# Latent attention: the reciprocals of the softmax sums spread over rows by two fp32r products of ones with diagonal blocks, in place of plain fp32 products

## The chip, the cores and the metric

One core of a Trainium2 chip runs the whole program. The metric is the device time of that core in microseconds (us), lower is better. Before the change three runs gave 3945.37, 3948.91 and 3950.83 us, median 3948.91.

## What is computed

A two-layer backbone over 1024 latent and 256 context tokens. Each layer runs three head groups side by side (a long convolution, retention, latent attention), an output projection and an MLP. The change touches only the attention with its 8 heads:

```python
s = jnp.einsum('bqhd,bkhd->bhqk', qi, k, preferred_element_type=jnp.float32)
p = jax.nn.softmax(s, axis=-1).astype(v.dtype)
return jnp.einsum('bhqk,bkhd->bqhd', p, v)
```

Keys and queries have 96 rows, values 64, keys are 1024 latent and 256 context tokens. In layer 0 context tokens are queries too (they see only the 256 context keys); in layer 1 they are not.

## The kernel before, in words

All products are made in "fp32r": an operand is split into a high part and a low part, each of which the TensorE takes at one pass, and three products (high by high, high by low, low by high) are summed in PSUM. They appear as L152, L153 and L154, the lines of the helper `three_pass`. A product of plain fp32 operands is taken by the TensorE as two instructions for one in the code.

`phase_latent` works on units (p, s, t): pair of heads p (0 to 3), head s in the pair, tile t of 128 queries. Layer 0 has 80 units (10 tiles, the last two of context), layer 1 has 64. Two units in a row are a couple, 72 couples in all. Each engine runs a loop over steps j and handles several units at different stages in it, in an order written out by hand:

- TensorE in step j: scores of unit j in two parts (512 and 768 keys); transposes of the probabilities of units j-2 and j-1 (L2031), which need a free PSUM bank of a ring of four; half of the products with the values of a couple (`weigh`, L2051); and, if the deck has one at this step, a product that makes keys, values or queries of the next pair (`make`). In odd steps `weigh` ends with the products of L2059.
- VectorE in step j: maximum of scores, part 0 (L1923); low parts of probabilities of unit j-2 (L1943); maximum, part 1 and the scaled maximum (L1927); the rest of the low parts; in odd steps `invert` (L1936 adds the two partial sums, L1937 takes the reciprocal).
- ScalarE: high parts of probabilities (L1767), copies of made products out of PSUM (L1748), the couple's output (L1775 to L1777), the exponentials (L1757).
- GpSimd (POOL in the profile): splits what was made into high and low parts (`split`, L1823 to L1847), converts the next pair's weights (`weights`, L1806 to L1809), and multiplies each couple's output by the reciprocals (`norm`, L1856 and L1859).

The softmax is divided by its sums at the very end. The sums of a couple lie as two columns of 128 partitions; the output lies with queries along its columns. So L2059 turns the reciprocals: the column, broadcast to 64 columns, is the stationary operand, the identity matrix the moving one, in plain fp32, once for each unit of the couple. The result, 64 rows of equal values, is copied out at L1775 as `att_rec`.

The semaphore `inverted` tells TensorE that a couple's reciprocals are there, `weighed` tells the others that its last product is done. `invert` of a couple is in VectorE's step 2m+3, the products that use it in TensorE's step 2m+5. `made_in` is the deck: in which step each of the next pair's keys, queries and values is made. It starts with step 5 of each pair's period of 20 (layer 0) or 16 (layer 1) steps and takes one item a step. The raw weights of the next pair are loaded by SyncE and converted by GpSimd in step 3 of a period.

Of the kernel before, what the change touches and what calls it, by code (L numbers as in the profile page):

```python
# [19 lines left out]
F32 = mybir.dt.float32  # L20
F32R = mybir.dt.float32r
ALU = mybir.AluOpType
# [3 lines left out]
P = 128  # L26
# [20 lines left out]
MLA_V = 64  # L47
# [35 lines left out]
class Chain:  # L83
# [6 lines left out]
    def link(self, eng, ins):  # L90
        self.count += 1
        ins.then_inc(self.sem, 1)
        eng.wait_ge(self.sem, self.count)
# [1441 lines left out]
LAT_QW, LAT_KVW = PAIR * HEAD_W, PAIR * (MLA_NOPE + MLA_V)  # L1535


def latent_weights(kit, l, q, p):


    first = p == 0
    uq_raw, ukv_raw = kit.at("uq_raw", [P, 2, LAT_QW], 187 if first else 130), kit.at("ukv_raw", [P, LAT_KVW], 191 if first else 132)
    w_raw = kit.sig("lat_w_raw", 16)
    q.dma_start(uq_raw[:], kit.io["mla_w_uq"][l, p].rearrange("(t p) n -> p t n", p=P)).then_inc(w_raw.sem, 16)
    q.dma_start(ukv_raw[:], kit.io["mla_w_ukv"][l, p]).then_inc(w_raw.sem, 16)
# [11 lines left out]
def phase_latent(kit, l):  # L1557
# [14 lines left out]
    SUM_RING, Q_SLOTS, RAWS = 8, 3, 2  # L1572
    uq_raw = [kit.at("uq_raw", [P, 2, LAT_QW], kb) for kb in (187, 130)]
    ukv_raw = [kit.at("ukv_raw", [P, LAT_KVW], kb) for kb in (191, 132)]
    rot, rope_part = kit.at("rope_rows", [P, SEQ], 70), kit.at("rope_part", [P, 2, 512], 193)
# [14 lines left out]
    kr = kr_wide[:, KR_AHEAD:, :]  # L1590
# [3 lines left out]

    mx = kit.at("att_max", [P, 2, 8], 202.5)
    sums, rinv = kit.at("att_sums", [P, 2, SUM_RING], 202.75), kit.at("att_rinv", [P, SUM_RING], 203)
    psf = ps[:].rearrange("p a b -> p (a b)")
    SCALE = MLA_QK ** -0.5
    T_BANK, T_RING, O0 = 3, 4, 7 * 512
# [6 lines left out]
    per_pair = PAIR * per_head  # L1606
# [20 lines left out]
    for p in range(1, PAIRS):  # L1627
        deck = [("k", p, 0, c) for c in range(3)] + queries(p, 0) + [("v", p, 0, c) for c in range(3)] + queries(p, 1)
        made_in.update({(p - 1) * per_pair + 5 + i: m for i, m in enumerate(deck)})
    later_makes = [made_in[j] for j in sorted(made_in)]  # L1630
# [38 lines left out]
    kr_ready = kit.sig("lat_kr_ready")  # L1669
# [29 lines left out]
    with nc.Block() as block:  # L1699
        @block.sync  # L1700
        def _(sp):
            sp.dma_start(rot[MLA_NOPE:P, :], io["rope_rows"]).then_inc(rot_in.sem, 16)
            sp.wait_ge(kr_ready.sem, kr_ready["kr"])
            latent_weights(kit, l, sp, 1)
            n_tok = len(q_tiles) * P
            for p in range(PAIRS):
                if p + 2 < PAIRS:
                    sp.wait_ge(w_lo.sem, w_lo[p + 1])
                    latent_weights(kit, l, sp, p + 2)
                sp.wait_ge(normed.sem, normed[num[(p, PAIR - 1, q_tiles[-1])] // 2])  # L1710
                row = 2 * HY_W + p * P
                sp.dma_start(kit.cat_dram[row:row + P, 0:n_tok], att[:, p % 2, 0:n_tok]).then_inc(stored[p % 2].sem, 16)
            for s in range(2):
                sp.wait_ge(stored[s].sem, stored[s].total)
# [161 lines left out]
        def _(dve):  # L1876
            link = kit.dve_chain.link
            dve.wait_ge(w_hi.sem, w_hi["first"])
            dve.tensor_tensor(ukvl[:], ukv_raw[0][:], ukvh[:].bitcast(F32), ALU.subtract)
# [50 lines left out]
            def invert(m):  # L1930

                n_parts, at = len(keys(units[2 * m])), 2 * m % SUM_RING
                dve.wait_ge(exped.sem, exped[(2 * m + 1, n_parts - 1)])
                total = sums[:, 0, at:at + 2]
                if n_parts == 2:
                    link(dve, dve.tensor_tensor(total, total, sums[:, 1, at:at + 2], ALU.add))  # L1936
                dve.reciprocal(rinv[:, at:at + 2], total).then_inc(inverted.sem, 1)  # L1937

# [30 lines left out]
        def _(pe):  # L1969
# [65 lines left out]
            def weigh(m, half):  # L2035
# [17 lines left out]
                if half == 1:  # L2053

                    pe.wait_ge(inverted.sem, inverted[m])
                    r = s * MLA_V
                    for i in range(2):
                        at = (2 * m + i) % SUM_RING
                        last = pe.matmul(psf[r:r + MLA_V, O0 + (2 + i) * P:O0 + (3 + i) * P],  # L2059
                                         rinv[:, at:at + 1].broadcast_to([P, MLA_V]), kit.ident[:], start=True, stop=True)  # L2060
                    last.then_inc(weighed.sem, 1)
# [1011 lines left out]
def build(nc, io, phases=None):  # L3073
    with ExitStack() as ctx:
# [5 lines left out]
        kit.stat = kit.small("stat", [P, 4, 20])  # L3080
        kit.ones = kit.small("ones", [P, P])
        kit.mla_gain = kit.small("mla_gain", [P, 3])
# [4 lines left out]
        kit.ret_gcol = kit.small("ret_gcol", [P, DEPTH, RET_H])  # L3087
        kit.ret_pos, kit.ret_lg = kit.small("ret_pos", [P, 4]), kit.small("ret_lg", [P, 8, DEPTH * 2 * RET_H])
        kit.ret_dm_dram = nc.dram_tensor("ret_dm_scratch", (DEPTH, P, RET_H, P), F32).ap()
        kit.spec_dram = [nc.dram_tensor("spec_scratch", (DEPTH, P, SEQ // 2 // P, 2, 4 * HY_W), F32).ap(),  # L3090
# [130 lines left out]
```

## Time and profile before

| | before |
|---|---|
| median of three runs | 3948.91 us |
| the profiled execution | 3948.27 us, of which the span is 3946.4 us |
| TensorE busy | 3643.4 us (92%) |
| VectorE busy | 2129.9 us (54%) |
| ScalarE busy | 1417.4 us (36%) |
| GpSimd busy | 1366.5 us (35%) |
| mean granted TensorE clock | 0.946 of full |

The span runs from the first to the last instruction; 1.9 us lie around it. Busy times are sums of the spans of instructions. In a row of the timeline the first number is the start in us from the span's start, the second how long the piece took, then engine, line, operation, output and inputs with their shapes, how many instructions were merged, and in square brackets the idle time of that engine before it with what ended it.

### The profile page before, as it was taken

Reading aid. Unit: us, or ns where it says so; the run is one execution under the profiler, and the core shown is the slowest. Engines: PE = TensorE matmul, PEld = TensorE weight load, DVE = VectorE, ACT = ScalarE, POOL = GpSimd, SP = SyncE. Lnnn points to the kernel's source line nnn. Section 1 sums busy time; section 2 is a strip of 40 time slices with the busy share of each in tenths; the row PEclk is TensorE's granted clock in tenths of the full one; section 3 lists DMA queues with packets and bytes.
Section 4 is the critical chain, followed back from the end, with each engine's and each line's share of the span. In section 5 each row is a group of like instructions: output and inputs, shape, how many; then the busy total and the mean of one; then the engine's idle time right before and its main releaser. Section 6 shows DMA issues by size and latency. Waiting matters only on the chain. (4 is left out here: it accounts for less than half of the span.)

```text
span 3946.4 us, 53247 instructions
## 1 busy us (share of the span) xinstructions
PE 3643.4 (92%) x19584; PEld 3058.6 (78%) x19584; DVE 2129.9 (54%) x3793; ACT 1417.4 (36%) x2845; POOL 1366.5 (35%) x1239
## 2 busy tenths in 40 slices
PE   7989997999779899999999899969996989999997
PEld 3668996777667688888888679958886768888886
DVE  5468435666676444444444583356676555544544
ACT  3341125666513522222222412246672252222222
POOL 1121122555100055454554421126630005544554
PEclk8989977999889999999999899879998999999999
DMA  5245201001324111111111162010014311111111
GB/s 206 104 168 186 82 4 41 12 8 40 122 78 163 43 43 32 32 43 43 43 32 32 69 202 79 4 39 10 6 39 165 150 43 50 52 48 43 53 52 49
DMA packets 153895, 266.96 MB, mean 68 GB/s; under 512 B 8968, under 2 KB 122777, under 8 KB 151290
## 3 DMA queue, kind: packets, MB, share of 16 engines
q1 hardware_dynamic: 143452, 212.38, 16.2%
q0 software_dynamic: 6352, 46.01, 3.0%
q10 hardware_dynamic: 3920, 6.29, 0.5%
q8 instruction: 107, 1.75, 0.2%
q14 instruction: 64, 0.52, 0.0%
HBM read 229.10 MB, written 33.59 MB: 67 GB/s over the span
## 5 line engine op out<-in xcount | busy, mean ns | idle before, releaser
L2990 POOL TENSOR_TENSOR x<-x,mlp_tmp 128x512 f32<-128x512 f32 x576 | 785.3, 1394 | 1323.7 <-DVE mlp_tmp L2971 1318.5
L2971 DVE TENSOR_TENSOR mlp_tmp<-psum,gate 128x512 f32<-128x512 f32 x576 | 391.7, 689 | 273.1 <-POOL x L2990 194.5
L152 PE MATMUL psum<-act_hi,w_hi 128*128 128x512 f32 (+1 forms) x1280 | 472.6, 369 | 14.4 <-DVE w_lo L2949 14.4
L153 PE MATMUL psum<-act_lo,w_hi 128*128 128x512 f32 (+1 forms) x1280 | 472.3, 369 | 0.0
L154 PE MATMUL psum<-act_hi,w_lo 128*128 128x512 f32 (+1 forms) x1280 | 472.1, 369 | 0.0
L152 PE MATMUL psum<-w_hi,hidden_hi 128*128 128x512 f32 x1152 | 449.9, 391 | 0.0
L153 PE MATMUL psum<-w_lo,hidden_hi 128*128 128x512 f32 x1152 | 448.5, 389 | 0.0
L154 PE MATMUL psum<-w_hi,hidden_lo 128*128 128x512 f32 x1152 | 448.3, 389 | 0.0
L2963 DVE TENSOR_TENSOR hidden_lo<-square,hidden_hi 128x512 fp32r<-128x512 f32 x160 | 102.3, 639 | 591.9 <-ACT hidden_hi L2935 591.9
L1923 DVE TENSOR_REDUCE att_max<-psum 128x1 f32<-128x512 f32 (+2 forms) x272 | 217.4, 799 | 259.7 <-PE psum L154 259.5
L2927 ACT ACTIVATE relu<-psum 128x512 f32<-128x512 f32 x160 | 88.8, 555 | 666.0 <-PE psum L154 666.0
L152 PEld LDWEIGHTS psum<-act_hi,w_hi 128*128 128x128 f32 x1280 | 242.2, 189 | 56.0 <-DVE w_lo L2949 15.2
L1757 ACT ACTIVATE probs<-psum,att_max 128x512 f32<-128x512 f32 (+2 forms) x272 | 208.5, 771 | 190.5 <-DVE att_max L1927 189.8
L153 PEld LDWEIGHTS psum<-act_lo,w_hi 128*128 128x128 f32 x1280 | 242.2, 189 | 40.6
L154 PEld LDWEIGHTS psum<-act_hi,w_lo 128*128 128x128 f32 x1280 | 242.2, 189 | 40.3
L152 PE MATMUL psum<-w_in_hi,act_hi 128*128 128x256 f32 (+1 forms) x912 | 259.2, 284 | 0.0
L154 PE MATMUL psum<-w_in_hi,act_lo 128*128 128x256 f32 (+1 forms) x912 | 256.8, 282 | 0.0
L153 PE MATMUL psum<-w_in_lo,act_hi 128*128 128x256 f32 (+1 forms) x912 | 256.8, 282 | 0.0
L152 PEld LDWEIGHTS psum<-w_hi,hidden_hi 128*128 128x128 f32 x1152 | 216.3, 188 | 47.6 <-DVE mlp_tmp L2971 3.6
L154 PEld LDWEIGHTS psum<-w_hi,hidden_lo 128*128 128x128 f32 x1152 | 216.3, 188 | 45.2
L153 PEld LDWEIGHTS psum<-w_lo,hidden_hi 128*128 128x128 f32 x1152 | 216.4, 188 | 43.7
L2923 ACT ACTIVATE w_hi<-w_raw 128x1024 fp32r<-128x1024 f32 x64 | 64.2, 1051 | 467.5 <-PE psum L154 467.5
(386 smaller groups left out, 8238.6 us busy)
## 6 DMA issues: line engine op xcount, KB each, us to landing
w_raw<-in_mlp_w SPq DMA_DIRECT2D x128, 512.0 KB, 3.8
side_w<-in_w_ada SPq DMA_DIRECT2D x40, 1024.0 KB, 6.5
w_raw<-in_w_in SPq DMA_DIRECT2D x32, 512.0 KB, 4.8
hy_ahead<-in_hy_ahead POOLq DMA_DIRECT2D x8, 2048.0 KB, 12.6
open_tab<-in_hy_ahead POOLq DMA_DIRECT2D x8, 1024.0 KB, 13.0
spec_scratch<-open_staged SPq DMA_DIRECT2D x16, 512.0 KB, 2.7
hy_spec<-spec_scratch SPq DMA_DIRECT2D x16, 512.0 KB, 3.5
hy_back<-in_hy_back POOLq DMA_DIRECT2D x2, 4096.0 KB, 29.9
```

The lines of the kernel that those rows point to most:

```text
L152: pe.matmul(out, lhs[0], rhs[0], start=start, stop=False)
L153: pe.matmul(out, lhs[0], rhs[1], start=False, stop=False)
L154: return pe.matmul(out, lhs[1], rhs[0], start=False, stop=stop)
L1757: act.activation(pe_[:, n % 2, at:end], psf[:, at:end], ACT.Exp, scale=SCALE, bias=mx[:, n % 2, 1:2], accum_out=sums[:, k, n % SUM_RING:n ...
L1923: dve_last = dve.tensor_reduce(mx[:, n % 2, 6 + k:7 + k], psf[:, at:at + len(part) * P], AX.X, ALU.max)
L2923: act.activation(w2h[:, f], raw2[:, f], ACT.Copy).then_inc(w2_hi.sem, 1)
L2927: act.activation(relu[:, i % 2, 0:n], ps[:, i % 4, 0:n], ACT.Relu).then_inc(relued.sem, 1)
L2963: dve.tensor_tensor(hlo[:, g % 2, f, 0:n], square[:, i % 2, 0:n], hh[:, g % 2, f, 0:n].bitcast(F32), ALU.subtract).then_inc(h_lo.sem, 1)
L2971: dve.tensor_tensor(tmp[:, j % 2, :], ps[:, 4 + j % 4, :], gate[:, int(t >= LAT_TILES), 512 * h:512 * h + 512], ALU.mult).then_inc(gated.s ...
L2990: pool.tensor_tensor(a, a, tmp[:, j % 2, :], ALU.add).then_inc(added.sem, 1)
```

## The change

The reciprocals are spread by products of another kind. VectorE now builds, for each couple, a diagonal block from the identity and each reciprocal column, in a high and a low part (`diag`, two instructions each of 128 by 128, two sets in turn); TensorE multiplies a constant 128 by 128 block of ones (`ones_r`, fp32r) with the high and then the low part of both blocks at once, 256 columns each. `inverted` is signalled after the last of VectorE's four new instructions. To make room, the small tiles `att_max`, `att_sums` and `att_rinv` move to the constants' area, `ones` shrinks, the raw weights move onto the place of the tile that `split` uses as `turned_rows` and `other_hi`, so that SyncE waits for the last split of queries before it loads them, and the deck starts at step 6 instead of 5.

```diff
+    diag = [[kit.at(f"att_diag{a}", [P, 2, P], kb + a, F32R) for a in range(2)] for kb in (202, 131)]
...
-        made_in.update({(p - 1) * per_pair + 5 + i: m for i, m in enumerate(deck)})
+        made_in.update({(p - 1) * per_pair + 6 + i: m for i, m in enumerate(deck)})
...
-            sp.wait_ge(kr_ready.sem, kr_ready["kr"])
+            sp.wait_ge(lo_p.sem, lo_p[weights_free(1)])
             latent_weights(kit, l, sp, 1)
...
-                    sp.wait_ge(w_lo.sem, w_lo[p + 1])
+                    sp.wait_ge(lo_p.sem, lo_p[weights_free(p + 2)])
                     latent_weights(kit, l, sp, p + 2)
...
+            link(dve, dve.memset(kit.ones_r[:].bitcast(F32), 1.0))
...
-                dve.reciprocal(rinv[:, at:at + 2], total).then_inc(inverted.sem, 1)
+                link(dve, dve.reciprocal(rinv[:, at:at + 2], total))
+                hi, lo = diag[m % 2]
+                if m >= 2:
+                    dve.wait_ge(weighed.sem, weighed[m - 2])
+                for i in range(2):
+                    last = dve.tensor_scalar(hi[:, i, :], kit.ident[:], rinv[:, at + i:at + i + 1], None, ALU.mult)
+                link(dve, last)
+                for i in range(2):
+                    last = dve.scalar_tensor_tensor(out=lo[:, i, :], in0=kit.ident[:], scalar=rinv[:, at + i:at + i + 1],
+                                                    in1=hi[:, i, :].bitcast(F32), op0=ALU.mult, op1=ALU.subtract)
+                last.then_inc(inverted.sem, 1)
...
-                    r = s * MLA_V
-                    for i in range(2):
-                        at = (2 * m + i) % SUM_RING
-                        last = pe.matmul(psf[r:r + MLA_V, O0 + (2 + i) * P:O0 + (3 + i) * P],
-                                         rinv[:, at:at + 1].broadcast_to([P, MLA_V]), kit.ident[:], start=True, stop=True)
+                    for a in range(2):
+                        last = pe.matmul(psf[:, O0 + 2 * P:O0 + 4 * P], kit.ones_r[:],
+                                         diag[m % 2][a][:].rearrange("p i n -> p (i n)"), start=a == 0, stop=a == 1)
                     last.then_inc(weighed.sem, 1)
```

`link` makes the engine wait for its own instruction before the next one.

## Rows read from the trace of the kernel before

**Rows 1.** Busy time by engine in both attention stages; columns: stretch, PE, PEld, DVE, ACT, POOL, PEclk, DMA.

```profile
655.00:1047.00 392.00, 362.79 (x2357) 306.93 (x2355) 242.40 (x504) 257.58 (x649) 202.57 (x237) 0.99 0.05 16
2622.00:2973.00 351.00, 336.77 (x2185) 285.97 (x2185) 227.65 (x448) 234.83 (x573) 184.82 (x209) 0.99 0.05 18
```

**Rows 2.** Timeline of a couple of layer 1 without a product of the deck.

```profile
2721.20 0.28 PE L2051 MATMUL psum<-probsT_hi,v_parts 128*128 128x256 f32 x1
2721.32 0.28 PE L2051 MATMUL psum<-probsT_lo,v_parts 128*128 128x256 f32 x1
...
2721.53 0.65 PE L2059 MATMUL psum<-ident,att_rinv 128*64 128x128 f32 x4
...
2722.11 0.50 PE L152 MATMUL psum<-kT_hi,qT_hi 96*128 96x512 f32 x1
...
2723.12 0.69 DVE L1923 TENSOR_REDUCE att_max<-psum 128x1 f32<-128x512 f32 x1 [1.15 <-PE psum L154]
```

**Rows 3.** Timeline of a couple of layer 1 with a product of the deck.

```profile
2677.95 0.69 DVE L1923 TENSOR_REDUCE att_max<-psum 128x1 f32<-128x512 f32 x1 [2.68 <-PE psum L154]
...
2679.38 1.23 PE L2031 MATMUL psum<-ident,probs 128*128 128x128 f32 x8 [0.20 <-DVE probsT_lo L1943]
```

**Rows 4.** Timeline of a couple of layer 0 where TensorE waits for the exponentials.

```profile
874.71 0.50 PE L152 MATMUL psum<-kT_hi,qT_hi 96*128 96x512 f32 x1 [0.41 <-ACT probs L1757]
...
875.70 0.69 DVE L1923 TENSOR_REDUCE att_max<-psum 128x1 f32<-128x512 f32 x1 [0.67 <-PE psum L154]
```

**Rows 5.** Groups of VectorE instructions by form: count, busy us, mean ns, idle before.

```profile
L851 DVE SCALAR_TENSOR_TENSOR side_acc<-side_w,cond,side_acc 128x256 f32<-128x256 f32 x560 | 229.0, 478 | 0.0
L1015 DVE TENSOR_SCALAR lat_xn<-mla,stat 128x128 f32<-128x128 f32 x18 | 5.8, 320 | 0.0
```

**Rows 6.** Timeline of VectorE, two neighbours of 128x128 in SBUF.

```profile
636.83 0.29 DVE L1524 TENSOR_TENSOR k_rope_tmp<-mla,rope 128x128 f32<-128x128 f32 x1
637.03 0.28 DVE L1525 TENSOR_TENSOR k_rope_tmp<-mla,rope 128x128 f32<-128x128 f32 x1
```

**Rows 7.** Line 1936: ns min/median/max; and one of it beside a POOL instruction.

```profile
L1936 DVE TENSOR_TENSOR att_sums<-att_sums x64: 147/151/873, 672.2 to 2967.5; 128x2 f32<-128x2 f32 x64
...
2673.77 1.28 POOL L1842 TENSOR_TENSOR make_raw<-make_raw,rope_rows 32x512 f32<-32x512 f32 x1
...
2674.44 0.63 DVE L1936 TENSOR_TENSOR att_sums<-att_sums 128x2 f32<-128x2 f32 x1
```

**Rows 8.** Timeline of POOL and VectorE around 2375 us.

```profile
2375.47 2.58 POOL L1223 TENSOR_TENSOR w_in_lo<-w_raw,w_in_hi 128x1024 fp32r<-128x1024 f32 x1 [23.44 <-ACT w_in_hi L1169]
2378.01 2.58 POOL L1223 TENSOR_TENSOR w_in_lo<-w_raw,w_in_hi 128x1024 fp32r<-128x1024 f32 x1
...
2375.73 2.60 DVE L851 SCALAR_TENSOR_TENSOR side_acc<-side_w,cond,side_acc 128x256 f32<-128x256 f32 x1
2378.26 2.62 DVE L851 SCALAR_TENSOR_TENSOR side_acc<-side_w,cond,side_acc 128x256 f32<-128x256 f32 x1
```

**Rows 9.** Timeline of POOL and VectorE around 228 us.

```profile
228.15 1.12 POOL L1042 CAST act_hi<-norm_tmp 128x512 fp32r<-128x512 f32 x1 [1.39 <-ACT norm_tmp L976]
228.72 1.10 DVE L1015 TENSOR_SCALAR norm_xn<-x,stat 128x1024 f32<-128x1024 f32 x1
```

**Rows 10.** POOL's splitting instructions by line: ns min/median/max, forms.

```profile
L1830 POOL CAST kT_hi<-make_raw x18: 390/603/649, 689.0 to 2844.9; 64x512 fp32r<-64x512 f32 x12, 64x256 fp32r<-64x256 f32 x6
L1847 POOL TENSOR_TENSOR qT_lo<-make_raw,qT_hi x35: 721/1277/1296, 664.8 to 2893.4; 96x512 fp32r<-96x512 f32 x28, 96x256 fp32r<-96x256 f32 x7
```

**Rows 11.** Weights of the second pair in layer 1: loads of `uq_raw`, end of conversion, first product.

```profile
DMA to landing us min/median/max: 2.7/3.0/3.9
...
2643.40 0.40 POOL L1806 CAST w_ukv_hi<-ukv_raw 128x256 fp32r<-128x256 f32 x1
...
2652.52 0.50 PE L152 MATMUL psum<-lat_hi,w_ukv_hi 128*128 128x512 f32 x1
```

**Rows 12.** Timeline of POOL at 532 us, while VectorE runs thirteen instructions in a row.

```profile
532.48 8.24 POOL L1441 TENSOR_TENSOR ret_state<-ret_state,ret_gcol 64x256 f32<-64x256 f32 x1
```

More of the change, by code:

```diff
@@ L1541, in latent_weights @@
     first = p == 0
-    uq_raw, ukv_raw = kit.at("uq_raw", [P, 2, LAT_QW], 187 if first else 130), kit.at("ukv_raw", [P, LAT_KVW], 191 if first else 132)
+    uq_raw, ukv_raw = kit.at("uq_raw", [P, 2, LAT_QW], 187 if first else 133), kit.at("ukv_raw", [P, LAT_KVW], 191 if first else 130)
     w_raw = kit.sig("lat_w_raw", 16)
@@ L1572, in phase_latent @@
     SUM_RING, Q_SLOTS, RAWS = 8, 3, 2
-    uq_raw = [kit.at("uq_raw", [P, 2, LAT_QW], kb) for kb in (187, 130)]
-    ukv_raw = [kit.at("ukv_raw", [P, LAT_KVW], kb) for kb in (191, 132)]
+    uq_raw = [kit.at("uq_raw", [P, 2, LAT_QW], kb) for kb in (187, 133)]
+    ukv_raw = [kit.at("ukv_raw", [P, LAT_KVW], kb) for kb in (191, 130)]
     rot, rope_part = kit.at("rope_rows", [P, SEQ], 70), kit.at("rope_part", [P, 2, 512], 193)
@@ L1593, in phase_latent @@
     o_hi, o_lo, o_rec = (kit.at(n, [P, 2 * P], kb) for n, kb in (("att_o_hi", 135), ("att_o_lo", 136), ("att_rec", 197)))
-    mx = kit.at("att_max", [P, 2, 8], 202.5)
-    sums, rinv = kit.at("att_sums", [P, 2, SUM_RING], 202.75), kit.at("att_rinv", [P, SUM_RING], 203)
+    mx, sums, rinv = kit.att_max, kit.att_sums, kit.att_rinv
+    diag = [[kit.at(f"att_diag{a}", [P, 2, P], kb + a, F32R) for a in range(2)] for kb in (202, 131)]
     psf = ps[:].rearrange("p a b -> p (a b)")
@@ L3080, in build @@
         kit.stat = kit.small("stat", [P, 4, 20])
-        kit.ones = kit.small("ones", [P, P])
+        kit.ones = kit.small("ones", [P, 8])
         kit.mla_gain = kit.small("mla_gain", [P, 3])
@@ L3088, in build @@
         kit.ret_pos, kit.ret_lg = kit.small("ret_pos", [P, 4]), kit.small("ret_lg", [P, 8, DEPTH * 2 * RET_H])
+        kit.att_max, kit.att_sums, kit.att_rinv = (kit.small(n, s) for n, s in (
+            ("att_max", [P, 2, 8]), ("att_sums", [P, 2, 8]), ("att_rinv", [P, 8])))
+        kit.ones_r = kit.small("ones_r", [P, P], F32R)
         kit.ret_dm_dram = nc.dram_tensor("ret_dm_scratch", (DEPTH, P, RET_H, P), F32).ap()
```

## The prediction, made before the change was run

> **What bounds the kernel now.** I read the busy times by stretch first, then the timeline of single couples, then every place where VectorE and GpSimd meet. In both attention stages TensorE is busy 93% and 96% of the time at a granted clock of 0.99, VectorE 62% and 65%, GpSimd just over half [rows 1]. So TensorE sets the pace, but not alone. The timeline shows three kinds of couple. Without a product of the deck (most of layer 1's second half) TensorE hardly waits, and VectorE stands idle 1.15 us between its reciprocal and the next maximum [rows 2]. With a product VectorE's idle time there is longer, 2.68 us here [rows 3], from 1.0 to 3.6 over all such couples; yet TensorE already waits 0.20 us for VectorE's low parts in the same step, because a transposition needs the PSUM bank that they free. In four couples of layer 0 TensorE waits 0.41 us for exponentials right after L2059, and VectorE's idle time is 0.67 us [rows 4]. That idle time before L1923 is the cover of anything added to `invert`.
>
> **What TensorE gains.** Two products in code are four instructions a couple (two for each product, two products). The last L2051 starts at 2721.32, the next product after L2059 at 2722.11: 0.79 us [rows 2]. Neighbouring L2051, which have the new products' shape (128x128 stationary, 256 columns, fp32r), start 0.12 apart in the same rows [rows 2]. Without L2059 the distance would be 0.12, so L2059 costs 0.67; two new products cost 2 x 0.12 = 0.24. The gain is 0.43 us a couple, 72 x 0.43 = 31 us if nothing else were late. They read `ones_r` and `diag`, both long ready: `invert` runs two steps ahead of the products that use it, so `inverted` holds up nobody even if it comes 5 us later. VectorE's new wait, for `weighed` of two couples back, is equally covered; behind it are queued the four new instructions and the next maximum, and it would cost them only if TensorE fell back a whole couple of 9 us.
>
> **What VectorE gets.** Four instructions of 128x128, with a link after the reciprocal and one between the pairs. No such form stands in the attention. Nearest rows: a tensor_scalar of 128x128 takes 0.32 at the mean [rows 5], a two-input one 0.29 with its neighbour starting 0.20 after it [rows 6]; scalar_tensor_tensor of 256 columns has 229.0/560 = 0.41 from start to start and 0.48 long [rows 5], less 128 columns at about 1 ns each 0.28 and 0.35. A link costs about 0.04. In sum 0.04 + 0.20 + 0.28 + 0.04 + 0.28 + 0.35 = 1.2 us. Bounds: 0.9 (all at the spacing of [rows 6], shortest ends) and 1.4 (no overlap at all). I take 1.2, since [rows 5, 6] are the same engine with operands in the same memory.
>
> TensorE now reaches the next scores 0.43 earlier, so VectorE is late by 1.2 + 0.43 less its idle time. Alone this costs 1.63 - 1.15 = 0.48 in a couple as in [rows 2], which takes back the whole 0.43; 1.63 - 0.67 = 0.96 in those of [rows 4], of which 0.43 was no gain to begin with. In some 30 couples with a product it would cost nothing. Over the 42 couples whose `invert` meets an idle GpSimd I count some 12 us late (14 of layer 1 at about 0.45, the rest in layer 0 between 0 and 0.9).
>
> **What VectorE meets.** The larger term. L1936, an instruction of two columns, takes 0.15 at the median but 0.87 at most [rows 7]. Of its 64 instances 23 take over 0.3, and each of these ends 0.02 after a GpSimd instruction: the one shown starts at 2674.44 and ends at 2675.07, GpSimd's ends at 2675.05. The instruction waits for GpSimd's to end. The new ones are of the kinds that do so: scalar_tensor_tensor with two inputs in SBUF waits 2.3 us for GpSimd [rows 8], tensor_scalar too [rows 9]. And it doesn't wait once. At 2375.47 GpSimd's instruction waits for the third L851, runs to 2378.05, the fourth L851 ends 0.28 after; meanwhile GpSimd's next came at 2378.01 and goes ahead of the fifth L851, which therefore takes 2.62 again [rows 8]. At 228 us the same with tensor_scalar: GpSimd 1.12 in place of 0.61, then VectorE 1.10 in place of 0.75 [rows 9]. They take turns, one instruction each. The Trainium skill says the same in "SBUF — State Buffer", section "SBUF: two separate sides": an instruction of either engine holds the shared port pair to its end and the other is fully blocked. In its section "Who interferes with whom" it adds that the order of issue decides who is blocked. That speaks against this change, and it excludes only a cost of nothing beside a busy GpSimd: the forecast and the rivals (a) and (b) all agree with it. It doesn't say who is next when both have one waiting; the rows do, for these two kinds.
>
> So where GpSimd has a chain of work, the four new instructions wait for half an instruction and three whole ones. Splitting queries or keys is casts of 0.61 and two-input instructions of 1.28 [rows 10] at a mean of 1.0: at most 3.5 us; in about a third of cases the chain ends sooner, which leaves 2.8. VectorE then needs 1.2 + 2.8 = 4.0 us against an idle time of 2.2 at the mean of these couples, late by 4.0 + 0.43 - 2.2 = 2.2. There are 23 + 7 such inverts (in seven more GpSimd began in the same instant), so 30 x 2.2 = 66 us. Nothing absorbs a late maximum in a step with a product: the low parts that TensorE already waits for come behind it [rows 3]. But every us lost lets GpSimd finish more of its chain before the next `invert`; for that I take off a fifth, 13 us, an estimate without a row of its own.
>
> **The rest.** GpSimd itself loses 4 x 0.3 us in these couples; its results are needed several steps later, hidden by that distance. The deck one step later moves no work off TensorE; it moves which GpSimd work `invert` meets, counted as a bound below. The second pair's weights are loaded after the last split of queries, where GpSimd now starts to convert (2643.40): two issues and a landing of 3.0 to 3.9 [rows 11] put it about 4.4 us later, its 3.3 us of work ends near 2651, and the first product that needs it moves from 2652.5 to a step later, 2658. Hidden by 7 us; without that cover it would cost 4.4 twice. SyncE has behind its wait only the store of `att`, which is not due for a pair. Later pairs load when the split ends, one or two steps before GpSimd's step 3. The memset of ones is 0.2 us while VectorE waits for ScalarE anyway. Smaller `ones` and moved tiles: nothing.
>
> **Sum.** -31 (TensorE) + 12 (late without GpSimd) + 66 - 13 (late with it) = +34; the deck's shift lays queries of 6 us, the longest splits, over one `invert` more in each period, 6 periods at about 1 us: +6. In all +40. On the profiled execution, 3948.27 + 40 = 3988. It lies 0.6 below the median of the three runs, which I neglect.
>
> **The rivals.**
> (a) VectorE keeps its turn: while both have work waiting, VectorE's neighbours go one after another and GpSimd gets in only at the two links. For it: at 532.48 one GpSimd instruction takes 8.24 us while thirteen of VectorE run through [rows 12]. Against it: [rows 8, 9]. Then half an instruction and one whole, 1.5 us: 2.7 + 0.43 - 2.2 = 0.9 late, 30 x 0.9 = 28; 28 + 12 - 31 = +9, less the catching up +5: 3953.
> (b) The other side: only the first new instruction waits (0.5 us), the rest run on. Late by 1.7 + 0.43 - 2.2, nearly nothing at the mean, some 6 us over all: 6 + 12 - 31 = -13, 3935. It decides where the time between reciprocal and maximum with GpSimd busy stays below about 2.6 us. Nothing in the trace shows an instruction of VectorE passing a waiting one of GpSimd except [rows 12].
> (c) Everything is hidden, VectorE's lateness doesn't reach TensorE: -31, 3917. Against it the 0.20 wait in [rows 3].
> (d) Worse than forecast: no catching up, and the deck's shift puts nearly every odd step of the deck over a full chain, 36 inverts with 3.5 us of waits: 36 x (1.2 + 3.5 + 0.43 - 2.2) = 105; 105 + 12 - 31 = +86, or +60 if it catches up by a quarter: 4008 to 4034.
>
> **How the numbers follow.** Forecast (taking turns, +20 to +60) 0.63; (d) 0.12; (a) 0.12; (b) 0.10; (c) 0.03. The likeliest's own range is 3968 to 4008. To leave out no more than 2 in 10 it takes in (a) and the better half of (d): 3946 to 4025. A measurement of this kernel tells about 0.2% or 8 us from no change: slower is the forecast, (d) and a part of (a), 0.79; the same is most of (a), 0.09; faster (b) and (c), 0.12, rounded.
>
> **What would show it.** In the timeline after: the two new products 0.12 apart and 0.36 from the last L2051 to the next; tensor_scalar and scalar_tensor_tensor at 0.2 to 0.35 where GpSimd is idle, and at 0.9 to 1.6, each ending just behind a GpSimd instruction, where it is busy. TensorE's waits for `probsT_lo` should grow by 30 us or more, in the steps of the deck, not in layer 1's last pair, which should stay within 1 us of before. If the new instructions have stretched only once a couple, (a) or (b) holds; if they stretch and TensorE's waits don't grow, (c).

## The result, and the profile after

The change makes the kernel slower: 3966.24 us at the median of six runs (3964.97 to 3967.82) against 3949.87 of the kernel before, measured beside it (six runs). The ratio is 1.0043, 95% interval 1.003 to 1.0055. The forecast was 3988: the sign was right, the loss is 16.4 us where 40 were forecast. The time lies inside the wide range of 3946 to 4025 and 2 us below the likeliest outcome's own range (3968 to 4008). The profiled execution spans 3963.1 us (before 3946.4).

Both attention stages again by engine, in the columns of [rows 1]; the stretches are laid over the same work, 10 and 6 us longer.

```profile
658.00:1060.00 402.00, 351.80 (x2282) 306.85 (x2280) 305.66 (x664) 258.82 (x649) 203.46 (x237) 0.97 0.05 17
2635.00:2992.00 357.00, 327.43 (x2121) 282.14 (x2121) 278.54 (x576) 235.79 (x575) 185.74 (x209) 0.98 0.05 18
```

VectorE has gone from 62% and 65% of the stretch to 76% and 78%. TensorE, which set the pace at 93% and 96%, is busy 88% and 92%: it waits more. And its granted clock, 0.99 in [rows 1], is 0.97 and 0.98. The groups of the new instructions, and who waits for what (out<-in, count | busy us, mean ns | idle us before them, what ended it):

```profile
L1924 DVE TENSOR_REDUCE att_max<-psum 128x1 f32<-128x512 f32 (+2 forms) x272 | 216.3, 795 | 161.7 <-PE psum L154 161.4
...
L2042 PE MATMUL psum<-ident,probs 128*128 128x128 f32 x1312 | 207.3, 279 | 56.7 <-DVE probsT_lo L1954 43.8 <-ACT probs L1757 12.7
...
L1946 DVE SCALAR_TENSOR_TENSOR att_diag<-ident,att_rinv,att_diag 128x128 fp32r<-128x128 f32 x144 | 75.9, 567 | 2.6
L1943 DVE TENSOR_SCALAR att_diag<-ident,att_rinv 128x128 fp32r<-128x128 f32 x144 | 48.0, 374 | 2.5
L2068 PE MATMUL psum<-att_diag,ones_r 128*128 128x256 f32 x144 | 28.6, 280 | 0.0
```

L2042 are the transpositions (L2031 before), L1954 the low parts (L1943 before), L1924 the maxima (L1923 before). TensorE's waits for low parts were 23.6 us before and are 43.8; those for exponentials at the transpositions grew from 0.2 to 12.7.

**A couple without a product of the deck**, to be held beside [rows 2]. The timeline's columns are start, duration, engine and line.

```profile
2666.82 0.28 PE L2062 MATMUL psum<-probsT_lo,v_parts 128*128 128x256 f32 x1
...
2666.94 0.40 PE L2068 MATMUL psum<-att_diag,ones_r 128*128 128x256 f32 x2
...
2667.18 0.48 PE L152 MATMUL psum<-kT_hi,qT_hi 96*128 96x512 f32 x1
...
2667.32 0.17 DVE L1938 RECIPROCAL att_rinv<-att_sums 128x2 f32<-128x2 f32 x1
...
2667.52 0.48 DVE L1943 TENSOR_SCALAR att_diag<-ident,att_rinv 128x128 fp32r<-128x128 f32 x2
...
2668.04 0.61 DVE L1946 SCALAR_TENSOR_TENSOR att_diag<-ident,att_rinv,att_diag 128x128 fp32r<-128x128 f32 x2
...
2668.57 0.68 DVE L1924 TENSOR_REDUCE att_max<-psum 128x1 f32<-128x512 f32 x1
```

From the last L2062 to the next product it is 0.36 us in place of 0.79: the forecast gain of 0.43. From the end of the reciprocal, 2667.49, to the end of the new work, 2668.65, it is 1.16 (forecast 1.2), and the maximum follows with no idle time.

**A couple whose `invert` meets a chain on GpSimd:**

```profile
2791.00 0.17 DVE L1938 RECIPROCAL att_rinv<-att_sums 128x2 f32<-128x2 f32 x1
2791.03 1.28 POOL L1841 TENSOR_TENSOR make_turned<-make_raw,rope_rows 32x512 f32<-32x512 f32 x1
...
2791.20 1.39 DVE L1943 TENSOR_SCALAR att_diag<-ident,att_rinv 128x128 fp32r<-128x128 f32 x2
...
2792.39 1.35 POOL L1842 TENSOR_TENSOR make_raw<-make_raw,rope_rows 32x512 f32<-32x512 f32 x1
...
2792.62 2.61 DVE L1946 SCALAR_TENSOR_TENSOR att_diag<-ident,att_rinv,att_diag 128x128 fp32r<-128x128 f32 x2
...
2793.82 1.27 POOL L1843 TENSOR_TENSOR make_raw<-make_raw,make_turned 32x512 f32<-32x512 f32 x1
...
2795.16 0.68 DVE L1924 TENSOR_REDUCE att_max<-psum 128x1 f32<-128x512 f32 x1
...
2796.58 0.63 PE L2042 MATMUL psum<-ident,probs 128*128 128x128 f32 x4 [2.05 <-DVE probsT_lo L1954]
```

The hi pair waits for L1841 and then runs through together, 1.39 in place of 0.48. L1842 gets in at the link; the first of the lo pair waits for it, L1843 gets in between the two, and the pair takes 2.61 in place of 0.61. So VectorE meets three GpSimd instructions, not four. Behind it the maximum is late, behind that the low parts, and TensorE waits 2.05 us.

Over all 72 couples, the time from the reciprocal's end to the end of the lo pair is 1.16 us in 43, and more by 45.0 us in all in the other 29: 1.55 us each at the mean, at most 2.9.

### The profile page after: what moved, and what is told of

The parts are those of the page before. It is cut to its first block and busy times, and to the rows that moved or that the text cites. A ratio compares the mean times of both kernels' runs of the same rounds, so it can differ in the third digit from the quotient of the medians.

```text
span 3963.1 us, 53319 instructions
## 1 busy us (share of the span) xinstructions
PE 3619.7 (91%) x19440; PEld 3051.3 (77%) x19440; DVE 2243.5 (57%) x4083; ACT 1420.0 (36%) x2845; POOL 1373.6 (35%) x1239
## 5 line engine op out<-in xcount | busy, mean ns | idle before, releaser
L1924 DVE TENSOR_REDUCE att_max<-psum 128x1 f32<-128x512 f32 (+2 forms) x272 | 216.3, 795 | 161.7 <-PE psum L154 161.4
L2042 PE MATMUL psum<-ident,probs 128*128 128x128 f32 x1312 | 207.3, 279 | 56.7 <-DVE probsT_lo L1954 43.8
L153 PEld LDWEIGHTS psum<-w_lo,hidden_hi 128*128 128x128 f32 x1152 | 216.3, 188 | 43.8
```

Source lines behind the costliest of these rows:

```text
L153: pe.matmul(out, lhs[0], rhs[1], start=False, stop=False)
L1924: dve_last = dve.tensor_reduce(mx[:, n % 2, 6 + k:7 + k], psf[:, at:at + len(part) * P], AX.X, ALU.max)
L2042: last = pe.transpose(bank[:, m * P:(m + 1) * P], pe_[:, n % 2, (at + m) * P:(at + m + 1) * P], kit.ident[:])
```

## The experiments

The edits stand against the changed kernel; their line numbers are a few off its own. All times are medians; each ratio is to the kernel before, run beside it. "Attention" is the distance in the profiled execution from the first unit's scaled maximum to the last one's, both layers added. It leaves out what the change doesn't touch (the stretch between the layers' attentions differs by up to 10 us between executions), and it is 715.3 before and 731.5 after: the 16.2 us are all of the loss. "At 1.2 GHz" is the time in it for which the granted clock was at the lower of its two levels, read in stretches of half a microsecond; "PE busy" is TensorE's busy time there. The last four columns each come from one execution of a kernel.

| kernel | us | ratio, 95% interval | attention | waits behind the reciprocal (couples) | at 1.2 GHz | PE busy |
|---|---|---|---|---|---|---|
| before | | | 715.3 | | 5.2 | 677.8 |
| e_shift | 3945.8 | 0.9995, 0.9986 to 1.0004 | 715.3 | | 8.8 | 677.6 |
| e_pe_only | 3916.8 | 0.9922, 0.9909 to 0.9934 | 684.0 | | 3.8 | 644.9 |
| e_dve_only | 3978.4 | 1.0068, 1.0054 to 1.0083 | 744.0 | 47.9 (29) | 32.9 | 687.7 |
| changed | 3966.2 | 1.0043, 1.003 to 1.0055 | 731.5 | 45.0 (29) | 29.3 | 659.0 |
| e_deck5 | 3968.5 | 1.0052, 1.0039 to 1.0065 | 739.4 | 47.4 (30) | 42.5 | 665.3 |
| e_all_nosplit | 3945.9 | 0.9983, 0.9974 to 0.9992 | 712.6 | 16.2 (12) | 25.8 | 657.3 |
| e_pe_nosplit | 3917.0 | 0.9913, 0.9898 to 0.9928 | 686.2 | | 8.8 | 647.0 |
| e_turns | 3986.4 | 1.0095, 1.0079 to 1.011 | 756.4 | 51.5 (27) | 65.2 | 671.8 |
| e_few | 3946.3 | 0.9989, 0.998 to 0.9998 | 709.9 | 30.5 (32) | 18.9 | 654.8 |
| e_lo_next | 3925.1 | 0.9933, 0.9919 to 0.9946 | 691.0 | 16.9 (25), hi pair only | 5.0 | 646.1 |
| e_lo_next_d5 | 3927.2 | 0.9946, 0.9932 to 0.996 | 697.4 | | 10.8 | 651.1 |
| e_all_next | 3945.3 | 0.9991, 0.9982 to 1.0 | 711.8 | | 3.9 | 648.1 |
| e_few_next | 3926.1 | 0.9938, 0.9925 to 0.9952 | 692.2 | | 5.2 | 648.4 |

### One part at a time

The deck and the placement alone, the kernel after with these lines as before:

```diff
-                link(dve, dve.reciprocal(rinv[:, at:at + 2], total))
-                hi, lo = diag[m % 2]
...
+                dve.reciprocal(rinv[:, at:at + 2], total).then_inc(inverted.sem, 1)
...
-                    for a in range(2):
-                        last = pe.matmul(psf[:, O0 + 2 * P:O0 + 4 * P], kit.ones_r[:],
...
+                                         rinv[:, at:at + 1].broadcast_to([P, MLA_V]), kit.ident[:], start=True, stop=True)
```

> The changed kernel without its new computation: the four plain products and the bare reciprocal of before, with only the placement of the raw weights, their later loads and the deck one step later. Theory A (the loss comes from the added VectorE work and its waits for the port): the deck is worth about +6 us, so 3952 to 3960 us, ratio 1.0005 to 1.0025. Theory B (the deck is what costs: the last product of a period now meets the queries' GpSimd splits under a reciprocal): 3966 us or more, ratio at least 1.004, with units 34 to 40 of a period slower as in the changed kernel.

The ratio is 0.9995 and the attention takes 715.3 us, to the tenth what it took before. That is below the range of theory A too. Theory B falls, and the forecast's +6 for the deck with it: beside the old work the later deck costs nothing.

> The changed kernel with its deck put back on the steps of before. Theory A: about the deck's +6 us less than the changed kernel, 3958 to 3964 us, ratio 1.002 to 1.0035. Theory B: the whole loss goes, under 3950 us, ratio below 1.000. A third case: the deck's place was chosen for the port, and without it the waits grow, over 3970 us, ratio above 1.005.

```diff
-        made_in.update({(p - 1) * per_pair + 6 + i: m for i, m in enumerate(deck)})
+        made_in.update({(p - 1) * per_pair + 5 + i: m for i, m in enumerate(deck)})
```

Neither A nor B; the third case comes nearest (the ratio is 1.0052, the waits grow from 45.0 to 47.4 us), though the time stays under its 3970. Beside the new VectorE work the old steps are no better, and perhaps worse: 2 us by the medians, with intervals that overlap, and 7.9 by the attention of one execution, in which the lower clock alone makes 6.6 (half of 13.2 us more). The loss isn't in the deck.

> TensorE's part alone: the two fp32r products read blocks that are made only for the first two couples of a layer (the identity itself), and VectorE does its reciprocal and nothing more; what is left out is the scaling of the outputs. Placement, loads and deck as in the changed kernel. Theory A: 72 x 0.43 us = 31 us less than the same kernel with the old products, that is 3921 to 3930 us, ratio 0.993 to 0.995. If TensorE's gain is swallowed by waits for VectorE and ScalarE, less than half of it shows: over 3940 us.

```diff
-                for i in range(2):
-                    last = dve.tensor_scalar(hi[:, i, :], kit.ident[:], rinv[:, at + i:at + i + 1], None, ALU.mult)
...
+                if m < 2:
+                    for a in range(2):
+                        for i in range(2):
+                            link(dve, last)
+                            last = dve.tensor_copy(diag[m][a][:, i, :], kit.ident[:])
```

The attention is 31.3 us shorter than in e_shift; 72 x 0.43 is 31.0. (The medians are 29.0 apart; 3916.8 lies 4 us below the range, which counted on +6 for the deck.) Nothing of TensorE's gain is swallowed while VectorE has no more to do than before. The changed kernel is 47.5 us behind this one: that is what VectorE's work costs beside the fast products.

> VectorE's part alone: it makes both blocks of each couple as in the changed kernel, nobody reads them, and TensorE does the four plain products of before. Output as the reference. Theory A: the terms add up, so the changed kernel's time plus the 31 us of TensorE: 3990 to 4000 us, ratio 1.0105 to 1.013. If VectorE's work is late only because TensorE became faster, part of it hides again: 3966 to 3980 us.

Only the products are put back, and 3978.4 lies in the range of the second case. VectorE's work costs 744.0 - 715.3 = 28.7 us here and 47.5 beside the fast products: the parts don't add up. Seen from TensorE, its 0.43 a couple is worth 31.3 us alone and 744.0 - 731.5 = 12.5 beside VectorE's work. The 0.43 us were cover for VectorE. The medians say the same, +28.8 and 12.2.

### Is it GpSimd, or mere length?

Both of these kernels leave out the splits of the third and fourth pair of heads:

```diff
                 pool.wait_ge(copied.sem, copied[m])
+                if p >= 2:
+                    pool.tensor_copy(other_hi[MLA_NOPE:P, 0:1], raw[MLA_NOPE:P, 0:1]).then_inc(lo_p.sem, 1)
+                    return
```

> The changed kernel, with GpSimd's splits of the raw products for the third and fourth pair of heads (the ones it does in the second and third period of each layer) left out: it copies one column and signals. To be read against e_pe_nosplit. Port theory: VectorE's added work costs 47.5 us in the attention's eight periods (changed kernel less the one with TensorE's part alone), 24.7 of it in the second and third periods; without GpSimd's splits these fall to the price of couples without a product, 0.33 us in each of 36 couples = 12 us, so 35 us in all. Rival (mere length: 1.1 us more on VectorE, late whatever GpSimd does): the difference stays at 45 to 50 us, the four periods at 22 to 25.

> TensorE's part alone, with the same splits left out. Since VectorE's slack covered its waits before, at most 5 us less than the same kernel with the splits: 3910 to 3918 us, ratio 0.990 to 0.992. The second and third periods then should read 94 to 95 and 84 us, as before.

By quarters of a layer's attention (a pair of heads each), in us; the splits are missing in the second and third:

```
                 layer 0                          layer 1
changed          106.58  102.58  102.58   81.95    91.76   89.02   88.99   68.08
e_pe_only         96.20   94.96   94.99   78.40    85.25   84.25   84.28   65.69
e_all_nosplit    106.56   96.26   96.30   83.94    91.75   85.39   84.88   67.52
e_pe_nosplit      97.54   94.95   94.93   78.42    86.25   84.19   84.20   65.70
```

With the splits VectorE's work costs 24.7 us in the four middle quarters (7.62 + 7.59 + 4.77 + 4.71); without them 4.6 (1.31 + 1.37 + 1.20 + 0.68). Everywhere else the instructions are the same. So four fifths of that cost are GpSimd's, and the rival of mere length falls. (This cost holds what the clock adds behind a wait: twice in these quarters it falls to 1.2 GHz in the changed kernel, never in e_all_nosplit.) The waits behind the reciprocal agree: 16.2 us in 12 couples are left, in the other quarters. The 12 us forecast for what remains was too much: a couple with a product in it has the slack for 1.16 us. The last quarters, which have neither products nor splits, give length its price: 3.55 + 2.39 us over 18 couples (in e_all_nosplit layer 0's reads 2.0 longer; it has two drops of the clock where the changed kernel has one).

### Who gets in where

> The changed kernel with its four instructions in the order hi, lo, hi, lo in place of hi, hi, lo, lo; one more of them waits for the one ahead of it. If GpSimd gets in at each place where VectorE waits for its own result, and between two of the longer form, the waits behind the reciprocal grow from 45 us toward 60 to 70 and the time by as much: 3980 to 3990 us, ratio 1.0075 to 1.010. If the number of instructions alone sets them (four as before), they stay at 45 us and the kernel within 5 us of 3966; the plain length grows by at most 0.1 us a couple.

```diff
                 for i in range(2):
-                    last = dve.tensor_scalar(hi[:, i, :], kit.ident[:], rinv[:, at + i:at + i + 1], None, ALU.mult)
-                link(dve, last)
-                for i in range(2):
+                    link(dve, dve.tensor_scalar(hi[:, i, :], kit.ident[:], rinv[:, at + i:at + i + 1], None, ALU.mult))
```

The total is the forecast one, 3986.4; the way to it only half. VectorE and GpSimd in its timeline:

```profile
857.98 0.17 DVE L1938 RECIPROCAL att_rinv<-att_sums 128x2 f32<-128x2 f32 x1
...
858.01 1.27 POOL L1841 TENSOR_TENSOR make_turned<-make_raw,rope_rows 32x512 f32<-32x512 f32 x1
...
858.18 1.18 DVE L1943 TENSOR_SCALAR att_diag<-ident,att_rinv 128x128 fp32r<-128x128 f32 x1
...
859.36 1.26 POOL L1842 TENSOR_TENSOR make_raw<-make_raw,rope_rows 32x512 f32<-32x512 f32 x1
859.40 1.37 DVE L1944 SCALAR_TENSOR_TENSOR att_diag<-ident,att_rinv,att_diag 128x128 fp32r<-128x128 f32 x1
...
860.69 1.35 DVE L1943 TENSOR_SCALAR att_diag<-ident,att_rinv 128x128 fp32r<-128x128 f32 x1
860.70 1.26 POOL L1843 TENSOR_TENSOR make_raw<-make_raw,make_turned 32x512 f32<-32x512 f32 x1
...
862.01 0.61 POOL L1846 CAST qT_hi<-make_raw 96x512 fp32r<-96x512 f32 x1
862.07 0.69 DVE L1944 SCALAR_TENSOR_TENSOR att_diag<-ident,att_rinv,att_diag 128x128 fp32r<-128x128 f32 x1
```

Now every one of the four waits, each behind one more GpSimd instruction: the strict turns of the forecast, 3.4 us at most in a couple against its 3.5. The tensor_scalar that rode along behind its neighbour in the changed kernel has lost its ride. But the waits over all couples are 51.5 us, not 60 to 70, and the undisturbed work is 0.13 longer (1.29, above the bound of 0.1 that I set), 9 us over 72 couples. These two are at most 16 of the 24.9 us that the attention grew. The rest shows in the last two columns of the table: 35.9 us more at 1.2 GHz, 12.8 us more of busy TensorE for the same products.

> The blocks made by one product of 128x512 (the identity times a broadcast column) in place of four of 128x128, the column's hi and lo parts split before in two instructions of 128x2. The column's split costs 0.3 to 0.4 us, the large one an estimated 0.6 to 0.7, so 1.0 us behind the reciprocal as before. If each instruction's turn at the port is what costs, one long turn in place of four: 3950 to 3960 us, ratio 1.000 to 1.0025. If length alone counts, 3963 to 3969 us. A product with a broadcast that runs at half the speed would make it 3980 us or more.

```diff
...
+                link(dve, dve.tensor_copy(both[:, 0, :], rinv[:, at:at + 2]))
+                link(dve, dve.tensor_tensor(both[:, 1, :], rinv[:, at:at + 2], both[:, 0, :].bitcast(F32), ALU.subtract))
+                dve.tensor_tensor(diag[m % 2][:].rearrange("p a i n -> p (a i) n"),
+                                  kit.ident[:].rearrange("p (o n) -> p o n", o=1).broadcast_to([P, 4, P]),
...
```

```profile
747.30 0.17 DVE L1938 RECIPROCAL att_rinv<-att_sums 128x2 f32<-128x2 f32 x1
...
747.32 1.27 POOL L1841 TENSOR_TENSOR make_turned<-make_raw,rope_rows 32x512 f32<-32x512 f32 x1
...
747.50 1.12 DVE L1942 CAST att_split<-att_rinv 128x2 fp32r<-128x2 f32 x1
...
748.66 0.16 DVE L1943 TENSOR_TENSOR att_split<-att_rinv,att_split 128x2 fp32r<-128x2 f32 x1
748.67 1.27 POOL L1842 TENSOR_TENSOR make_raw<-make_raw,rope_rows 32x512 f32<-32x512 f32 x1
748.85 1.65 DVE L1944 TENSOR_TENSOR att_diag<-ident,att_split 128x512 fp32r<-128x512 f32 x1
```

Two waits where the changed kernel has three in the same place, and for instructions of any size: the 128x2 cast waits 1 us as a 128x128 one would. Undisturbed the work takes 1.12 us, as good as before the edit, yet the kernel is 20 us faster than the changed one, 4 us below the range of the theory of turns, and a little below the kernel before. At equal length, fewer instructions met GpSimd: waits 30.5 in place of 45.0, and half of the 10.4 us less at 1.2 GHz is 5.2 more.

### The place

```diff
+                if 0 <= j - 4 and j % 2 == 0 and j - 3 < n_units:
+                    invert_lo((j - 4) // 2)
```

> The lo pair moved to the end of VectorE's next step, behind that unit's maxima and probabilities, ahead of the TensorE step that reads it; the hi pair stays. If what costs is that the next first maximum comes late behind four instructions, the delay halves: of the 47.5 us about 20 go, 3940 to 3952 us, ratio 0.998 to 1.0005, and waits of TensorE for VectorE's lo probabilities fall from 43.7 us toward 25. If the cost is VectorE's total of work or GpSimd's hold of the port wherever the instructions stand, it stays within 4 us of the changed kernel's 3966.

```profile
2674.14 0.17 DVE L1940 RECIPROCAL att_rinv<-att_sums 128x2 f32<-128x2 f32 x1
...
2674.16 1.28 POOL L1843 TENSOR_TENSOR make_turned<-make_raw,rope_rows 32x512 f32<-32x512 f32 x1
...
2674.34 1.38 DVE L1945 TENSOR_SCALAR att_diag<-ident,att_rinv 128x128 fp32r<-128x128 f32 x2
...
2676.40 0.69 DVE L1926 TENSOR_REDUCE att_max<-psum 128x1 f32<-128x512 f32 x1 [0.68 <-PE psum L154]
...
2677.84 1.22 PE L2052 MATMUL psum<-ident,probs 128*128 128x128 f32 x8 [0.20 <-DVE probsT_lo L1962]
...
2679.65 1.56 DVE L1954 SCALAR_TENSOR_TENSOR att_diag<-ident,att_rinv,att_diag 128x128 fp32r<-128x128 f32 x2
```

3925.1 us, 0.7% faster than the kernel before. The hi pair still waits (1.38), but the maximum still comes 0.68 us after VectorE is free, and TensorE's wait is the 0.20 of [rows 3]. The lo pair waits for GpSimd as well (1.56), where the time shows little of it. VectorE does every instruction of the changed kernel, and they cost 7.0 us in place of 47.5. The cost lay in having all four together between the reciprocal and the next maximum, and the gain is twice the 20 us that I expected of halving the delay. Part of that is the clock again: 5.0 us at the lower level in place of 29.3. This edit both moves work and splits it over two places; the next one only moves it.

> Both pairs, hi and lo, moved to the end of VectorE's next step; only the sum and the reciprocal stay where they are. If the place is all that costs, the 7.0 us that VectorE's work still costs with the lo pair moved go too: 3916 to 3923 us, ratio 0.991 to 0.993, and TensorE's waits for the lo probabilities stand near the 20 us of the kernel with TensorE's part alone. If the next step has room for 0.65 us but not for 1.16, the maximum of the step after it is late in its turn: up to 0.5 us in 72 couples, so 3925 to 3955 us.

3945.3 us lies in the range of the room theory: the end of the next step has no room for all four. The end of one such group on VectorE, and what follows:

```profile
2672.19 2.63 DVE L1953 SCALAR_TENSOR_TENSOR att_diag<-ident,att_rinv,att_diag 128x128 fp32r<-128x128 f32 x2
...
2673.40 1.28 POOL L1844 TENSOR_TENSOR make_raw<-make_raw,rope_rows 32x512 f32<-32x512 f32 x1
...
2674.75 0.68 DVE L1926 TENSOR_REDUCE att_max<-psum 128x1 f32<-128x512 f32 x1
...
2676.17 1.23 PE L2051 MATMUL psum<-ident,probs 128*128 128x128 f32 x8 [0.78 <-DVE probsT_lo L1961]
```

TensorE's waits for low parts are 43.3 us, as in the changed kernel, but none is over 1.7, and the clock stays up: 3.9 us at 1.2 GHz. The kernel takes 21 us less than the changed one. But the room theory's reason, a length of 1.16 us in place of 0.65, isn't what fills the room, as the next kernel shows: here the undisturbed group is 1.12 us, and over 72 couples the groups take 75.3 us more than that, for GpSimd is at work there too.

> The column split and the one 128x512 product, all at the end of VectorE's next step. Shorter waits for the port than with four instructions; by the place theory the same 3916 to 3923 us as e_all_next, by the room theory 3920 to 3945 us, below e_all_next.

> The lo pair moved, and the deck on the steps of before. The deck's step was worth 0 (old products) and -2 us (changed kernel) so far: within 4 us of the 3925 us with the later deck, 3921 to 3932 us. If the later deck is what makes room at the end of the next step, over 3935 us.

Both times, 3926.1 and 3927.2, lie in the ranges given. The first tells more than I had asked of it. The same couple as above, in e_few_next:

```profile
2668.50 1.68 DVE L1951 TENSOR_TENSOR att_diag<-ident,att_split 128x512 fp32r<-128x512 f32 x1
...
2670.53 0.69 DVE L1926 TENSOR_REDUCE att_max<-psum 128x1 f32<-128x512 f32 x1 [0.35 <-PE psum L154]
...
2671.96 1.22 PE L2050 MATMUL psum<-ident,probs 128*128 128x128 f32 x8 [0.20 <-DVE probsT_lo L1960]
```

The work stands in the place of e_all_next and is as long when undisturbed (1.08 us against 1.12), yet over e_pe_only it costs 8.2 us of attention where e_all_next costs 27.8. So length doesn't fill the room. In the last quarters, without splits, the two cost 2.6 and 3.6 us; the rest, 5.6 and 24.2, lies where GpSimd has splits to do, and over all couples the groups are 38.1 and 75.3 us longer than undisturbed. That points to the waits for GpSimd, which fewer instructions meet less often; e_all_next without splits, which would show it by an edit, wasn't run. Splitting the work over two places and doing it in fewer instructions in one place are worth the same. The deck is worth 2 us by the medians, which the intervals don't separate from nothing.

## Why the prediction was half right

**TensorE's gain: right.** 0.43 us a couple in the timeline, 31.3 us in e_pe_only against the 31 of the sum.

**VectorE's length, and its price alone: right.** 1.16 us against 1.2. The last quarters, without products and splits, cost 3.55 + 2.39 us over 18 couples; less 1.7 for the one drop of the clock in them (below), that is 0.24 a couple, or 10 us over the 43 couples that met no GpSimd, and 7 to 8 if those outside the last quarters cost 0.13 each, as in the middle quarters of e_all_nosplit (4.6 us over 36). The sum had 12 over 42.

**The waits for the port: right in kind, place and count, wrong in size.** This is the step that failed. The prediction had 30 couples and the trace has 29, and e_all_nosplit shows that the waits are GpSimd's. But "half an instruction and three whole ones", 2.8 us, was taken from pairs of [rows 8, 9], and the trace has 1.55. Two things make the difference. The second tensor_scalar doesn't wait for a turn of its own, so that at most 2.9 us come together where the forecast had 3.5. And most waits end sooner than I assumed: of the 29, eleven are under 0.8 us, six 1.4 and only twelve over 2. My own rival (a) had nearly this size: at the 1.5 us that it assumed ("GpSimd gets in only at the two links"), I wrote 28 us for this term and 3953 in all. The truth lay between (a) and the forecast, with (a)'s rule for the hi pair and the forecast's for the lo pair. Between bounds of 0.5 and 3.5 us a value from the middle would have been nearer than one built on four strict turns.

**What follows a wait.** What is left of the 47.5 us after 10 for length and 13 for the clock is 24 to 25 us, 0.54 of the 45.0 us of waits. The forecast let 53 of 84 through, 0.63: the idle time was weighed about right, the waits were nearly twice too long. The 24 is a remainder, no measurement of its own, and the share isn't fixed: the same subtraction leaves 8 us for the 30.5 of e_few.

**The clock: not in the sum at all.** These are stretches of the changed kernel around one of its three longest waits, in the columns of [rows 1], and the wait itself in the timeline, after and before:

```profile
750.00:753.00 3.00, 3.00 (x26) 2.81 (x24) 2.90 (x6) 2.30 (x6) 2.84 (x3) 1.00 0.00 0
753.00:756.00 3.00, 0.04 (x1) 0.00 (x0) 2.96 (x5) 2.02 (x6) 2.78 (x4) 1.00 0.00 0
756.00:759.00 3.00, 1.68 (x10) 1.54 (x11) 2.06 (x5) 1.16 (x4) 2.76 (x4) 0.83 0.00 0
759.00:762.00 3.00, 3.00 (x18) 3.00 (x18) 0.33 (x1) 0.70 (x2) 1.57 (x3) 0.60 0.08 17
762.00:765.00 3.00, 3.00 (x22) 2.75 (x21) 2.86 (x11) 2.26 (x7) 0.00 (x0) 1.00 0.35 120
...
757.32 1.65 PE L2042 MATMUL psum<-ident,probs 128*128 128x128 f32 x8 [4.27 <-ACT probs L1757]
...
752.20 0.63 PE L2031 MATMUL psum<-ident,probs 128*128 128x128 f32 x4 [0.80 <-DVE probsT_lo L1943]
```

VectorE waits 0.9 us with the hi pair and 1.95 with the lo pair, TensorE stands 4.27 us from 753.0 on, where it waited 0.80 in the kernel before, and when it starts again its granted clock falls to 1.2 GHz: 18 products in 3 us where 26 ran before. The three waits over 4 us all fall where the unit in work is one of context queries: TensorE then has three score products of 256 columns and two transpositions to do while VectorE is late. I had taken the mean idle time, 2.2 us, for all these couples. Each of the three has such a drop behind it, of the shorter ones some have (one of 1.55 and two of 2.09) and some haven't (the 2.05 at 2796.58 above); in e_all_next none of the seven idle stretches of 1.5 to 1.7 has. In e_dve_only, e_deck5, e_turns and e_few all 26 waits of 2.1 us and more have one, behind them or already toward their end. Each kernel has a drop across the start of each stage, and some have another 10 to 16 us into it. In all the changed kernel has 29.3 us at the lower level where e_pe_only has 3.8. Half of the 25.5 is lost, 12.7; TensorE's busy time grew by 14.1. Not all of it is due to VectorE's work: two of the changed kernel's eight further drops, 6.8 us, are those 10 to 16 us into a stage, which e_shift and e_pe_nosplit have as well and e_pe_only happens not to have. Without them the loss is 9. The Trainium skill, "TensorE: Matmul & The Clock Gate", section "Terms", puts the penalty at the throttled time times the share of the clock that is held back, one half here; this trace agrees, 12.7 us against 14.1. The other kernels follow the same line roughly: e_deck5 20.4 us more busy than e_pe_only with half of 38.7 more at 1.2 GHz, e_turns 26.9 with half of 61.4, e_few 9.9 with half of 15.1, e_lo_next 1.2 with half of 1.2, and e_dve_only 10.1 us more than e_shift with half of 24.1. No run kept TensorE busy through a wait, so this term is read from busy time and granted clock in these kernels, not from an edit of its own.

**The deck: wrong.** The sum had +6. It is 0 with the old work (e_shift) and 0 or less with the new (e_deck5): -2 by the medians, -8 by one execution. In layer 0's second quarter the changed kernel's couples of units 36 and 38 do lose 3.9 and 2.0 us against the kernel before, as the longer splits now meet the `invert` there, but those of 24, 28 and 34 gain 1.3 to 1.6 each. I had counted only the former.

**The weights: right.** They are converted later, and TensorE doesn't wait for them:

```profile
2659.68 0.40 POOL L1806 CAST w_ukv_hi<-ukv_raw 128x256 fp32r<-128x256 f32 x1 [3.17 <-issue]
...
2671.71 0.47 PE L152 MATMUL psum<-lat_hi,w_ukv_hi 128*128 128x512 f32 x1
```

**The sum, then.** -31 for TensorE, +10 for length, +24 for waits, +13 for the clock, 0 for the deck: +16, against -31 + 12 + 53 + 6. As the 24 is what the other terms leave, the sum comes out by construction; with 8 for length it would be some 27, and 3 of the 13 for the clock are the chance drops at the stages' starts. Either way the waits cost about half of the 53 forecast. Two errors had opposite signs: the missing clock hid a good part of the overcounted waits. Of the signs that the prediction named, TensorE's waits for `probsT_lo` grew by 20 us, not 30, with 12.5 more for exponentials, and the last pair of layer 1 stayed within 0.5 us.

## What to carry to other kernels

Work moved to an engine that is 62% busy is not free by that number: what counts is the idle time at the one place where it is put, and how many separate instructions it brings there while another engine shares its port. Price the same work at its neighbouring places, and in fewer instructions, before dropping it: here 47.5 us of cost became 7.0 by moving one pair of instructions by one step, and a loss of 0.4% became a gain of 0.7%. And a late engine in front of TensorE costs again in clock once the wait gets long: keep single waits short, even at an equal sum.

## What the runs showed of the hardware that I had not expected

- Two neighbours of tensor_scalar keep together when GpSimd has its next instruction coming (0.48 grows to 1.39, one wait); two of scalar_tensor_tensor let it in between (0.61 to 2.61, two waits). In the changed kernel the second tensor_scalar started at about 2792.3, just ahead of GpSimd's 2792.39. The Trainium skill, "SBUF — State Buffer", section "Who interferes with whom", says that the order of issue decides who is blocked; these rows fit it.
- A cast of two columns, 0.17 us alone, takes 1.12 beside GpSimd. The wait goes by the instruction, not by its size; the instruction of two columns behind it ran at once (0.16), the one of 512 behind that waited again.
- A product of 128x512 whose two inputs are both broadcast takes 0.69 us, and writes what four instructions of 128x128 write in 1.16 with their overlap; with the two small ones that it needs it is 1.12.
- TensorE's waits for low parts are 43.8 us in the changed kernel and 43.3 in e_all_next, yet the attention takes 19.7 us longer in the first. There single waits reach 4.3 us, here 1.7; there TensorE has 25.4 us more at 1.2 GHz, and 8.6 us more of waits for exponentials.
